# Seven block products in place of eight for the gate and up projections of six feed-forward networks, in split single precision

## The chip, the core and the metric

The kernel runs on one core of one Trainium2 chip. The metric is the device time of the whole program in microseconds. Nothing crosses cores. All data is 32-bit floating point in memory.

## The reference

A sequence of 512 tokens with 1024 channels goes through three layers. Each has a feed-forward network (FFN), a mixer, and a second FFN, so there are six FFNs and three mixers (pooling with latent attention, gated convolution, Fourier mixing with grouped attention), and a last norm.

```
def swiglu(x, w_gate, w_up, w_down):
    return (jax.nn.silu(x @ w_gate) * (x @ w_up)) @ w_down

x = x + 0.5 * swiglu(rms_norm(x, ffn1_norm), w_gate, w_up, w_down)
x = x + mixer(rms_norm(x, mix_norm))
x = x + 0.5 * swiglu(rms_norm(x, ffn2_norm), ...)
```

The inner width is 2816 for the first four FFNs and 2752 for the last two. Gate and up weights are 1024 x width, down weights width x 1024.

## The kernel before

The program runs in nine stages, s = 1 to 9: FFNs are 1, 3, 4, 6, 7 and 9, mixers 2, 5 and 8. Activations are kept with channels on partitions: X is 8 tiles of 128 channels x 512 tokens. A product is made exact enough by splitting each operand into a high part (rounded to the matmul's type) and a low part (the remainder), and adding three matmuls, low x high, high x low and high x high (`mm3`, L379 to L382). The norm's factor per token, r (tile rb), is multiplied in after the matmul; the gain per channel is in Xh and Xl.

Weights come as one long stream of chunks of up to 128 x 1024 numbers (512 KB), in the order in which TensorE wants them (`weight_stream`). SyncE issues one load after another into three raw buffers (`fetch`). ScalarE makes the high part (`high`, the activation on L773), VectorE the low part (`low`, L1126), each into one of three buffers wh and wl. Both engines call `use` at fixed places of their programs, and each call lets them split as far as two chunks ahead of the one in use. Every engine is a queue that is worked off in order; an instruction that waits holds all behind it.

An FFN of before (`ffn`, once for each engine) has 11 groups of 256 inner channels. A group is four chunks: gate for channels 0 to 511 and 512 to 1023 of x, then up in the same way. TensorE sums two 128 x 512 tiles of gate and two of up in four of the eight PSUM banks, the next group in the other four. VectorE multiplies gate by r, ScalarE takes SiLU, VectorE multiplies up by r and both together, ScalarE copies that to Hh and VectorE makes Hl. After all groups `residual` runs the down projection over 22 tiles of H, and the outcome is added to X with factor 0.5; there ScalarE and VectorE also make the next stage's Xh and Xl and the squares for its norm. The norm's statistics come early in the next stage: after the second chunk a matmul sums the squares over channels, VectorE makes the variance (tile small), GpSimd raises it to -0.5 (tile r), VectorE makes a diagonal matrix (tile diag), and TensorE spreads it over partitions after the third chunk, whence ScalarE copies rb. GpSimd does nothing else in an FFN.

Of the kernel before, what the change touches and what calls it, by code (L numbers as in the profile page):

```python
# [17 lines left out]
N_RAW = 3  # L18
AHEAD = 2
# [95 lines left out]
def chunks_ffn(wg, wu, wd):  # L115
    f, got = wg.shape[1], []
    for n0 in range(0, f, 256):
        n1 = min(f, n0 + 256)
        got += chunks(wg, 0, D, n0, n1, 4) + chunks(wu, 0, D, n0, n1, 4)
    return got + chunks_down(wd, f)  # L120


def weight_stream(a):

    got = []
    got += chunks_ffn(a["ffn1_w_gate"][0], a["ffn1_w_up"][0], a["ffn1_w_down"][0])
    wi = a["a_w_in"][0]
    for n0, n1 in ((0, 256), (256, 512), (896, 1024), (1024, 1184), (512, 768), (768, 896)):
        got += chunks(wi, 0, D, n0, n1, 8 if n1 - n0 == 128 else 4)
    got += chunks(a["a_w_pool"][0].rearrange("g c d -> (g c) d"), 0, 512, 0, 128)  # L130
    for n0 in (0, 512):
        got += chunks(a["a_w_kv_up"][0], 0, 256, n0, n0 + 512)
    got += chunks(a["a_w_q_up"][0], 0, 384, 0, 288)
    got += chunks(a["a_w_out"][0], 0, 512, 0, 256)
    for n0, n1 in ((288, 576), (576, 768)):
        got += chunks(a["a_w_q_up"][0], 0, 384, n0, n1)
    for k0 in (0, 512):
        for n0 in range(256 if k0 == 0 else 0, D, 256):
            got += chunks(a["a_w_out"][0], k0, k0 + 512, n0, n0 + 256)
    for w in ("ffn2", "ffn1"):  # L140
        l = 0 if w == "ffn2" else 1
        got += chunks_ffn(a[w + "_w_gate"][l], a[w + "_w_up"][l], a[w + "_w_down"][l])
    for m in range(KT):
        for part in (1, 2, 0):
            n0 = part * D + m * 128
            got += chunks(a["c_w_in"][0], 0, D, n0, n0 + 128, 8)
    got += chunks_down(a["c_w_out"][0], D)
    got += chunks_ffn(a["ffn2_w_gate"][1], a["ffn2_w_up"][1], a["ffn2_w_down"][1])
    got += chunks_ffn(a["ffn1_w_gate_2"], a["ffn1_w_up_2"], a["ffn1_w_down_2"])
    for n0 in (1024, 512, 768, 0, 256):  # L150
        got += chunks(a["w_in_2"], 0, D, n0, n0 + 256, 4)
    got += chunks(a["dft_c"], 0, 128, 0, 256)
    got += chunks(a["dft_cs"], 0, T, 0, T)
    got += chunks(a["dft_ss"], 0, T, 0, T)
    got += chunks(a["fnet_w_2"].rearrange("g c d -> (g c) d"), 0, 512, 0, 128)
    for k0 in (0, 512):
        for n0 in range(0, D, 256):
            got += chunks(a["w_out_2"], k0, k0 + 512, n0, n0 + 256)
    got += chunks_ffn(a["ffn2_w_gate_2"], a["ffn2_w_up_2"], a["ffn2_w_down_2"])
    return got  # L160


def build(nc, a, out):
    ctx = ExitStack()
    with ctx:
# [14 lines left out]
        raw_in = [Event(sem(f"raw_in{i}")) for i in range(N_RAW)]  # L180
# [3 lines left out]
        X = sb("X", [128, KT, T], F)  # L184
        Xh = sb("Xh", [128, KT, T], R)
        Xl = sb("Xl", [128, KT, T], R)
        raw = [sb(f"raw{i}", [128, CAP], F) for i in range(N_RAW)]
        wh = [sb(f"wh{i}", [128, CAP], R) for i in range(N_RAW)]
        wl = [sb(f"wl{i}", [128, CAP], R) for i in range(N_RAW)]
# [7 lines left out]
        rb = [sb(f"rb{i}", [128, T], F) for i in range(2)]  # L197
        sq = [sb(f"sq{i}", [128, T], F) for i in range(2)]
        acc = [sb(f"acc{i}", [128, T], F) for i in range(2)]
# [6 lines left out]
        def scope():  # L206
            place[0] = stage_base
# [6 lines left out]
        stream = weight_stream(a)  # L214

        def parts_of(n, bufs):
            parts, width, _ = stream[n]
            return [bufs[n % N_RAW][0:rows, k0 * width:(k0 + nk) * width] for rows, k0, nk, _ in parts]

        def views(n):  # L220

            _, width, nk = stream[n]
            return [b[n % N_RAW][:, 0:nk * width].rearrange("p (k n) -> p k n", n=width) for b in (wh, wl)]

# [3 lines left out]
        H = [sb(n, [128, 22, T], R) for n in ("Hh", "Hl")]  # L228
        ft = [sb(f"ft{i}", [128, T], F) for i in range(3)]

        scope()
        aRB = sb("a_RB", [128, 10, T], R)
        aQT = [sb(f"a_QT{i}", [128, 2, T], R) for i in range(2)]
        aKT = [sb(f"a_KT{i}", [128, 2, T], R) for i in range(2)]
        aVh, aVl = (sb(n, [128, 4, T], R) for n in ("a_Vh", "a_Vl"))
        aqtm, aktm = (sb(n, [128, 4, 8, 96], F) for n in ("a_qtm", "a_ktm"))
        aP3 = [sb(f"a_P{i}", [128, T], F) for i in range(3)]
        azf = [sb(f"a_zf{i}", [128, T], F) for i in range(2)]
        akrT = sb("a_krT", [32, T], F)
# [10 lines left out]
        aacc = [diag, acc[1]]  # L250
# [10 lines left out]

        scope()
        gRB = sb("g_RB", [128, 8, T], R)
        gKT = sb("g_KT", [128, 2, 2, T], R)
        gVh, gVl = (sb(n, [128, 4, 2, 2, 64], R) for n in ("g_Vh", "g_Vl"))
        gABh, gABl = (sb(n, [128, 4, 4, 256], R) for n in ("g_ABh", "g_ABl"))
        gQT = gABh[:, :, :, :].rearrange("p (i a) (b c) n -> p i (a b) (c n)", i=2, b=2)
        gqtm = sb("g_qtm", [128, 4, 8, 64], F)
# [16 lines left out]
        class Mixer:  # L285
# [3 lines left out]
            def __init__(self, s, causal, ahead, early, fill, P, tiles, stats):  # L289
                self.s, self.causal, self.ahead, self.early, self.fill = s, causal, ahead, early, fill  # L290
                self.P, (self.PTh, self.PTl) = P, tiles
# [18 lines left out]
        mA = Mixer(2, True, 8, 2, (0, 2), aP, (aRB[:, 0:4, :], aRB[:, 4:8, :]), (amx, anb, aL, aLi))  # L310
        mB = Mixer(8, False, 6, 1, (1, 3), gP, (gRB[:, 0:4, :], gRB[:, 4:8, :]), (gmx, gnb, gL, gLi))
# [1645 lines left out]
```

## Time and profile before

| | |
|---|---|
| median of 3 runs | 2810.42 us (2810.4 to 2812.13) |
| the profiled execution | 2811.45 us, span 2809.6 us |
| granted TensorE clock, mean | 0.997 |
| matmuls, and as many weight loads | 12580 |
| read from memory | 249.17 MB, 89 GB/s over the span |

A group of matmul rows has a busy time that counts the overlap of one matmul with the next; the pace of the stream is the distance of their starts. An FFN stage without its neighbours takes about 364 us, and the six together most of the span. The profiled execution is 1 us above the median.

### The profile page before, as it was taken

What the parts mean: (1) busy time and instruction counts of PE and PEld (TensorE: products, weight loads), DVE (VectorE), ACT (ScalarE), POOL (GpSimd) and SP (SyncE); (2) the same over time, 40 slices, a digit from 0 to 9 for tenths busy, and PEclk for the clock granted to TensorE, in tenths of its full rate; (3) what the DMA queues carried; (4) which work ended last, traced back from release to release, by engine and by line L of the source; (5) the groups of instructions that cost most, each with busy time, mean ns of one, the idle gap of its engine ahead of it and who ended that gap; (6) DMA issues with size and microseconds to landing.
All of it is one profiled execution on the core that took longest, in us unless ns stands there. A gap on an engine that the chain in (4) does not pass through costs nothing.

```text
span 2809.6 us, 31389 instructions
## 1 busy us (share of the span) xinstructions
PE 2766.3 (98%) x12580; PEld 2261.5 (80%) x12580; DVE 1331.8 (47%) x1895; ACT 908.2 (32%) x1286; POOL 130.3 (5%) x130
## 2 busy tenths in 40 slices
PE   8999999999999999999999999999999999999998
PEld 6888878888888888888888888888877877788776
DVE  5444358654443444434654444344443557544432
ACT  4222226542322223222233232223222346432221
POOL 0000005300000000000000000000000114000000
PEclk9999999999999999999999999999999999999999
DMA  4332232033323333333333333333322320233322
GB/s 152 99 98 91 91 86 77 24 89 103 95 92 96 96 98 90 101 96 96 98 90 98 98 90 98 92 95 91 105 85 89 92 81 23 61 103 100 90 84 70
DMA packets 282704, 253.30 MB, mean 90 GB/s; under 512 B 8384, under 2 KB 278848, under 8 KB 282560
## 3 DMA queue, kind: packets, MB, share of 16 engines
q1 hardware_dynamic: 282560, 251.30, 29.9%
q8 instruction: 101, 1.65, 0.2%
q14 instruction: 43, 0.35, 0.0%
HBM read 249.17 MB, written 2.10 MB: 89 GB/s over the span
## 4 chain that ended last, share of the span: by engine, by line
PE 82%; issue 13%; DVE 3%; ACT 2%; DMA 0%; SPq 0%; POOLq 0%; POOL 0%; DVEq 0%
PE bank L380 27%; PE bank L381 27%; PE bank L382 27%; PE bank L469 1%; DVE a_mx L1235 0%; PE bank L433 0%; PE bank L422 0%; DMA raw<-in_ffn_w_gate 0%; DVE wl L1126 0%; ACT Xh L804 0%; DVE a_nb L1142 0%; ACT wh L773 0%; DVE a_KT L1138 0%; ACT a_P L857 0%; DVE X L1135 0%
## 5 line engine op out<-in xcount | busy, mean ns | idle before, releaser
L1126 DVE TENSOR_TENSOR wl<-raw,wh 128x1024 fp32r<-128x1024 f32 (+6 forms) x498 | 573.9, 1166 | 976.2 <-ACT wh L773 975.3
L380 PE MATMUL bank<-Xh,wl 128*128 128x512 f32 x2544 | 997.6, 392 | 12.9 <-DVE wl L1126 10.6
L382 PE MATMUL bank<-Xh,wh 128*128 128x512 f32 x2544 | 992.0, 390 | 0.0
L381 PE MATMUL bank<-Xl,wh 128*128 128x512 f32 x2544 | 991.5, 390 | 0.0
L773 ACT ACTIVATE wh<-raw 128x1024 fp32r<-128x1024 f32 (+6 forms) x498 | 494.9, 1009 | 1001.3 <-PE bank L382 994.9
L380 PEld LDWEIGHTS bank<-Xh,wl 128*128 128x128 f32 x2544 | 476.3, 187 | 117.0 <-issue 12.6
L381 PEld LDWEIGHTS bank<-Xl,wh 128*128 128x128 f32 x2544 | 476.4, 187 | 102.9 <-issue 1.9
L382 PEld LDWEIGHTS bank<-Xh,wh 128*128 128x128 f32 x2544 | 476.1, 187 | 103.0
L380 PE MATMUL bank<-Hh,wl 128*128 128x512 f32 x1056 | 419.0, 397 | 0.0
L382 PE MATMUL bank<-Hh,wh 128*128 128x512 f32 x1056 | 417.0, 395 | 0.0
L381 PE MATMUL bank<-Hl,wh 128*128 128x512 f32 x1056 | 417.0, 395 | 0.0
L1135 DVE TENSOR_TENSOR ft<-bank,rb 128x512 f32<-128x512 f32 x264 | 181.6, 688 | 168.7 <-PE bank L382 117.8
L380 PEld LDWEIGHTS bank<-Hh,wl 128*128 128x128 f32 x1056 | 197.9, 187 | 54.3 <-issue 6.6
L382 PEld LDWEIGHTS bank<-Hh,wh 128*128 128x128 f32 x1056 | 197.9, 187 | 48.6
L381 PEld LDWEIGHTS bank<-Hl,wh 128*128 128x128 f32 x1056 | 197.9, 187 | 47.5
L804 ACT ACTIVATE Hh<-ft 128x512 fp32r<-128x512 f32 x132 | 83.8, 635 | 269.2 <-DVE ft L1135 269.2
L841 ACT ACTIVATE ft<-ft 128x512 f32<-128x512 f32 x132 | 83.6, 633 | 209.3 <-DVE ft L1135 209.2
L1135 DVE TENSOR_TENSOR Hl<-ft,Hh 128x512 fp32r<-128x512 f32 x132 | 91.4, 692 | 92.5 <-ACT Hh L804 92.5
L1135 DVE TENSOR_TENSOR ft<-ft,ft 128x512 f32<-128x512 f32 x132 | 91.4, 692 | 4.5
L1678 POOL TENSOR_TENSOR r<-small,half 128x4 f32<-128x4 f32 x10 | 10.1, 1014 | 1758.5 <-DVE small L1144 1758.5
L801 ACT ACTIVATE Xh<-X,par 128x512 fp32r<-128x512 f32 x64 | 46.0, 725 | 130.4 <-DVE X L1138 110.6
L1138 DVE SCALAR_TENSOR_TENSOR Xl<-X,par,Xh 128x512 fp32r<-128x512 f32 x64 | 47.6, 751 | 44.5 <-ACT Xh L801 44.5
(264 smaller groups left out, 1583.5 us busy)
## 6 DMA issues: line engine op xcount, KB each, us to landing
raw<-in_ffn_w_gate SPq DMA_DIRECT2D x128, 512.0 KB, 3.8
raw<-in_ffn_w_up SPq DMA_DIRECT2D x128, 512.0 KB, 3.9
raw<-in_ffn_w_down SPq DMA_DIRECT2D x114, 512.0 KB, 3.5
raw<-in_c_w_in SPq DMA_DIRECT2D x24, 512.0 KB, 3.7
raw<-in_w_in SPq DMA_DIRECT2D x10, 512.0 KB, 3.8
raw<-in_a_w_in SPq DMA_DIRECT2D x8, 512.0 KB, 3.8
raw<-in_a_w_out SPq DMA_DIRECT2D x8, 512.0 KB, 3.5
raw<-in_c_w_out SPq DMA_DIRECT2D x8, 512.0 KB, 3.5
```

The costliest lines, as they stand in the source:

```text
L380: e.matmul(o, ll, rh, start=start, stop=False)
L381: e.matmul(o, lh, rl, start=False, stop=False)
L382: i = e.matmul(o, lh, rh, start=False, stop=stop)
L469: e.transpose(bank[0:rows, t * 128:(t + 1) * 128], src, ident).then_inc(mm.up(name), 1)
L773: e.activation(hi, src, ACT.Copy).then_inc(whi.up(("w", n)), 1)
L801: e.activation(Xh[:, t, :], X[:, t, :], ACT.Copy, scale=col(gain, t)).then_inc(act.up(("xh", s, t)), 1)
L804: e.activation(dst, src, ACT.Copy, scale=scale).then_inc(act.up(*names), 1)
L841: e.activation(B[0:wd, :], A[0:wd, :], ACT.Silu).then_inc(act.up(("silu", s, ht)), 1)
L1126: e.tensor_tensor(lo, src, hi.bitcast(F), ALU.subtract).then_inc(wlo.up(("w", n)), 1)
L1135: e.tensor_tensor(dst, a, b, op).then_inc(dve.up(*names), 1)
L1138: e.scalar_tensor_tensor(dst, a, scalar, b, op0, op1).then_inc(dve.up(*names), 1)
L1678: e.tensor_tensor(dst, a, b, op).then_inc(pool.up(*names), 1)
```

## The change

For gate and up of an FFN the weights are seen as a block matrix: A11 and A12 are the gate weights of 256 inner channels for x channels 0 to 511 and 512 to 1023, A21 and A22 those of up. x is cut in the same way into channels (first and second half) and tokens (0 to 255, 256 to 511), blocks B11, B12, B21, B22. A product of 2 x 2 blocks has 8 block products; here it is made with 7, over sums of blocks (S1 to S4 of the weights, T1 to T4 of x) and with sums of results. The first of the 11 groups stays as it was. The ten others are "jobs"; each product has 4 k-tiles x 2 halves x 3 terms and 256 columns.

- x sums: ScalarE makes X times gain into ya and yb (8 copies), VectorE the four sums T1 to T4, and both their high and low parts, at the start of each FFN while the first group is on TensorE. T4 goes to a place in Xh and Xl.
- weight sums: host code stores the blocks of the ten jobs contiguously, 128 x 1024 numbers each (4 KB a partition). SyncE loads A11, A21 (for S1), A12, A11 or A21 (for S3) and A22 as plain loads, five per job. GpSimd issues transfers that add a block of memory onto a raw buffer: S1 = A21 + A22, then S2 = S1 + A11 and S4 = S2 + A12 in the same buffer after the split of what stood there, and S3. Six raw buffers, four wh and four wl.
- results: three PSUM banks a job (a, b, c). ScalarE seeds bank b with a copy of product 1 and takes three snapshots (snapC, snapU, snapV) between products; TensorE waits for them before products 2, 6, 7, 3 and 4. VectorE adds and multiplies by r in 8 operations of 512 columns. Product 1 of a job is made in the middle of the one before, but for the first jobs of the two runs, so that jobs 3 and 9 are "alone" with six products.
- the down projection is made in two parts: over 8 tiles of H after job 3, over 14 after job 9; H has 14 places for 22 tiles. Each part is added to X.
- the widths 2752 are padded with zeros to 2816. One buffer less each of rb and acc; the mixers' tiles move to other addresses. The ring for GpSimd's transfers is set to 1024 bytes a partition.

```
+PRODUCT = {1: ("a", "A11", "B11"), 2: ("b", "A12", "B21"), 3: ("c", "S4", "B22"), 4: ("a", "A22", "T4"),
+           5: ("c", "S1", "T1"), 6: ("a", "S2", "T2"), 7: ("a", "S3", "T3")}
+def products(i):
+    if alone(i):
+        return [(i, p) for p in (5, 6, 2, 7, 3, 4)]
+    return [(i, 5), (i, 2), (i, 6), (i + 1, 1), (i, 7), (i, 3), (i, 4)]
+SLOT = {"A11": (0, 0), "A12": (1, 1), "S3": (2, 2), "A22": (3, 3), "S1": (4, 5), "S2": (4, 5), "S4": (4, 5)}
+SUMS = {"S1": ("A21", "A22"), "S2": (None, "A11"), "S3": ("A11", "A21"), "S4": (None, "A12")}
...
+    def run(self, s, i0, i1):
+        self.product(s, i0, 1)
+        for i in range(i0, i1):
+            for j, p in products(i):
+                self.product(s, j, p)
+        self.load_block(s, i0, "A11")
+        self.load_block(s, i0, "S1")
+        self.load_block(s, i0, "A12")
+        for i in range(i0, i1):
+            if i + 1 < i1:
+                self.load_block(s, i + 1, "A11")
+            self.load_block(s, i, "S3")
+            if i + 1 < i1:
+                self.load_block(s, i + 1, "S1")
+            self.load_block(s, i, "A22")
+            if i + 1 < i1:
+                self.load_block(s, i + 1, "A12")
...
+            def product(s, i, p):
+                role, _, operand = PRODUCT[p]
+                n, h, l, _ = chunk()
+                no = job_bank(role, i)
+                bank = take(no, (role, s, i)) if p in (1, 5) else banks[no]
...
+                if p in (2, 6):
+                    w.wait_ge(act, ("seed", s, i))
+                elif p == 7:
+                    w.wait_ge(act, ("snapU", s, i))
+                elif p == 3:
+                    w.wait_ge(act, ("snapC", s, i))
+                elif p == 4:
+                    w.wait_ge(act, ("snapV", s, i))
...
+                for k in range(4):
+                    xh, xl = x_operand(k, operand, 0), x_operand(k, operand, 1)
+                    for m in range(2):
...
+                        e.matmul(o, l[:, k, sl], xh, start=start, stop=False, skip_group_check=True)
+                        e.matmul(o, h[:, k, sl], xl, start=False, stop=False, skip_group_check=True)
+                        ins = e.matmul(o, h[:, k, sl], xh, start=False, stop=last, skip_group_check=True)
```

ScalarE's part of a job; `use` splits the weights three products ahead:

```
+                def job(i):
+                    for j, p in products(i):
+                        if (j, p) == (i, 5):
+                            use()
+                            if i == 0 or alone(i - 1):
+                                seed(i)
+                            if i > 0 and not alone(i - 1):
+                                silu(i - 1, 1)
+                        elif (j, p) == products(i)[1]:
+                            use()
+                            if i > 0:
+                                w.wait_ge(dve, ("h", s, i - 1))
+                            snap(snapC, "c", i, "snapC", 5)
+                            if i > 0 and not alone(i - 1):
+                                tail(i - 1)
+                        elif (j, p) == products(i)[3 if not alone(i) else 2]:
+                            if i > 0:
+                                w.wait_ge(dve, ("right", s, i - 1))
+                            snap(snapU, "a", i, "snapU", 6)
+                            use()
+                        elif p == 7:
+                            use()
+                            if not alone(i):
+                                seed(i + 1)
+                            silu(i, 0)
+                        elif p == 3:
+                            snap(snapV, "a", i, "snapV", 7)
+                            use()
+                        else:
+                            use()
```

GpSimd's part of an FFN:

```
+            def ffn(s):
+                def add(name, i):
+                    base, added = SUMS[name]
+                    slot, landed = SLOT[name][i % 2], sum_event(name, i)
+                    if base:
+                        w.wait_ge(raw_in[slot], (name, s, i))
+                    else:
+                        before = "S1" if name == "S2" else "S2"
+                        w.wait_ge(landed, (before, s, i))
+                        w.wait_ge(wlo, ("w", stream.op_of[before, s, i]))
+                    e.dma_start(raw[slot][:, :], stream.block[s, i, added], accum_op=ALU.add).then_inc(landed.sem, 16)
...
+                norm(s)
+                add("S1", 0)
+                for i in range(JOBS):
+                    if i == EARLY + 1:
+                        add("S1", i)
+                    add("S3", i)
+                    if not alone(i):
+                        add("S1", i + 1)
+                    add("S2", i)
+                    add("S4", i)
```

## Rows read from the trace of the kernel before

**Rows 1.** The page: span, TensorE's busy time, the chain by engine.

```profile
span 2809.6 us, 31389 instructions
...
PE 2766.3 (98%) x12580; PEld 2261.5 (80%) x12580; DVE 1331.8 (47%) x1895; ACT 908.2 (32%) x1286; POOL 130.3 (5%) x130
...
PE 82%; issue 13%; DVE 3%; ACT 2%; DMA 0%; SPq 0%; POOLq 0%; POOL 0%; DVEq 0%
```

**Rows 2.** TensorE's waits, longest: total us, times, longest.

```profile
PE bank L380 <- DVE wl L1126: 10.6, 2, 9.9
```

**Rows 3.** Busy time by stretch: us, PE, PEld, DVE, ACT, POOL, clock, DMA share.

```profile
620.00:642.00 22.00, 22.00 (x99) 18.22 (x98) 10.17 (x12) 6.56 (x8) 0.00 (x0) 1.00 0.33 98
```

**Rows 4.** TensorE's timeline in gate/up: start, us, line, operation.

```profile
699.72 0.39 PE L382 MATMUL bank<-Xh,wh 128*128 128x512 f32 x1
...
705.84 0.39 PE L382 MATMUL bank<-Xh,wh 128*128 128x512 f32 x1
```

**Rows 5.** TensorE's timeline in stage 8, 256 columns.

```profile
2235.79 0.28 PE L382 MATMUL bank<-wh,Xh 128*128 128x256 f32 x1
...
2242.99 0.28 PE L382 MATMUL bank<-wh,Xh 128*128 128x256 f32 x1
...
2272.47 0.28 PE L380 MATMUL bank<-wh,g_RB 128*128 128x256 f32 x1
...
2277.91 0.28 PE L381 MATMUL bank<-wl,g_RB 128*128 128x256 f32 x1
```

**Rows 6.** TensorE's timeline, a matmul over 64 rows and the next.

```profile
2792.74 0.50 PE L380 MATMUL bank<-Hh,wl 64*128 64x512 f32 x1
2793.08 0.39 PE L381 MATMUL bank<-Hl,wh 64*128 64x512 f32 x1
```

**Rows 7.** Groups by form, 620 to 642: busy us, mean ns.

```profile
L1126 DVE TENSOR_TENSOR wl<-raw,wh 128x1024 fp32r<-128x1024 f32 x4 | 4.8, 1224 | 7.6 <-ACT wh L773 7.6
L773 ACT ACTIVATE wh<-raw 128x1024 fp32r<-128x1024 f32 x4 | 4.1, 1053 | 7.8 <-PE bank L382 7.8
L1135 DVE TENSOR_TENSOR ft<-bank,rb 128x512 f32<-128x512 f32 x4 | 2.8, 688 | 2.5 <-PE bank L382 1.8 <-ACT ft L841 0.8
...
L841 ACT ACTIVATE ft<-ft 128x512 f32<-128x512 f32 x2 | 1.3, 632 | 3.2 <-DVE ft L1135 3.2
```

**Rows 8.** VectorE's timeline at the start of stage 3.

```profile
587.56 0.16 DVE L1144 TENSOR_SCALAR small<-bank 128x4 f32<-128x4 f32 x1 [2.12 <-PE bank L422]
588.88 0.69 DVE L1135 TENSOR_TENSOR diag<-par,r 128x512 f32<-128x512 f32 x1 [1.16 <-POOL r L1678]
```

**Rows 9.** ScalarE's timeline there: rb, and the table load before SiLU.

```profile
594.02 0.60 ACT L804 ACTIVATE rb<-bank 128x512 f32<-128x512 f32 x1 [6.13 <-PE bank L433]
...
597.53 1.28 ACT L841 ACT_TABLE_LOAD   x1 [1.96 <-DVE ft L1135]
```

**Rows 10.** TensorE after its last down matmul, and two stretches with clock.

```profile
2795.97 1.02 PE L422 MATMUL bank<-ones,acc 128*128 128x1 f32 x8 [2.27 <-DVE acc L1135]
...
2796.00:2800.00 4.00, 1.93 (x9) 1.41 (x10) 0.86 (x2) 0.00 (x0) 1.01 (x1) 0.80 0.00 0
...
480.00:490.00 10.00, 8.40 (x45) 7.28 (x46) 7.66 (x31) 6.88 (x20) 9.34 (x10) 0.83 0.12 36
```

**Rows 11.** Transfers: two stretches, then issues with KB, us to landing.

```profile
10.00:12.00 2.00, 2.00 (x5) 1.61 (x6) 1.15 (x2) 1.00 (x2) 0.00 (x0) 1.00 1.06 417
12.00:14.00 2.00, 2.00 (x7) 1.56 (x7) 1.91 (x3) 2.00 (x5) 0.00 (x0) 1.00 1.01 389
...
raw<-in_ffn_w_gate SPq DMA_DIRECT2D x128, 512.0 KB, 3.8
...
par<-in_par SPq DMA_DIRECT2D x1, 763.5 KB, 8.6
...
gain<-in_par SPq DMA_DIRECT2D x1, 4.0 KB, 1.8
```

**Rows 12.** GpSimd's timeline, the norm of stage 3.

```profile
587.81 1.04 POOL L1678 TENSOR_TENSOR r<-small,half 128x4 f32<-128x4 f32 x1 [42.41 <-DVE small L1144]
```

More of the change, by code:

```diff
@@ L112, in chunks_down, with __init__ @@
     return [c for n0, n1, per in DOWN for c in chunks(w, 0, f, 128 * n0, 128 * n1, per)]
[L115 to L120, printed above, removed]
+class Load:
+    def __init__(self, name, slot, parts, width, after):
+        self.name, self.slot, self.parts, self.width, self.after = name, slot, parts, width, after
+class Weights:
+    def __init__(self, slot, load, total, parts, width, nk):
+        self.slot, self.load, self.total, self.parts, self.width, self.nk = slot, load, total, parts, width, nk
+        self.buf = self.before = self.stage = self.due = None
@@ L231, in build @@
+        aP3 = [sb(f"a_P{i}", [128, T], F) for i in range(3)]
+        assert place[0] <= at_XT
+        scope(at_XT)
+        aqtm, aktm = (sb(n, [128, 4, 8, 96], F) for n in ("a_qtm", "a_ktm"))
         scope()
+        aCh, aCl = (sb(n, [128, KT, T], R) for n in ("a_Ch", "a_Cl"))
         aRB = sb("a_RB", [128, 10, T], R)
@@ new lines, in ffn @@
+            def ffn(s):
+                hooks = [nothing, *stats(s, 7, 7)]
+                for side in ("gate", "up"):
+                    proj([(FIRST_BANK[side, m], (side, s, m)) for m in range(2)], [128, 128], KT, Xh, Xl, x_ready(s), hooks)
+                mm.also(("plain", s))
+                for i in range(JOBS):
+                    if i == 0 or i == EARLY + 1:
+                        product(s, i, 1)
+                    for j, p in products(i):
+                        product(s, j, p)
+                    if i == EARLY:
+                        down(s, 0)
@@ L777, in use @@
                     used[0] += 1
-                    while split[0] < min(used[0] + AHEAD, len(stream)):
+                    while split[0] < len(ops) and used[0] >= ops[split[0]].due:
                         high()
@@ L1130, in use @@
                     used[0] += 1
-                    while split[0] < min(used[0] + AHEAD, len(stream)):
+                    while split[0] < len(ops) and used[0] >= ops[split[0]].due:
                         low()
@@ new lines, in job @@
+                def job(i):
+                    before = i > 0 and not alone(i - 1)
+                    use()
+                    if before:
+                        first_half_h(i - 1)
+                        times_r(i - 1, 1)
+                    use()
+                    if before:
+                        second_half_h(i - 1)
+                    use()
+                    if alone(i):
+                        low_h(i - 1)
+                        use()
+                        left(i)
+                        use()
+                        times_r(i, 0)
+                        lower_right(i)
+                        use()
+                        right(i)
+                    else:
+                        left(i)
+                        use()
+                        if before:
+                            low_h(i - 1)
+                        use()
+                        times_r(i, 0)
+                        use()
+                        lower_right(i)
+                        use()
+                        right(i)
@@ L1839, in sync_program @@
             e.dma_start(par[:, :], a["par"]).then_inc(par_in.sem, 16)
-            for n in range(2, len(stream)):
-                fetch(n)
+            for load in stream.loads[2:]:
+                fetch(load)
             for t in range(KT):
```

607 lines of the change are left out of this document (440 added, 167 removed).

## The prediction

> **What bounds the kernel now.** I read the page's busy table and its chain first. TensorE is busy for 2766.3 of 2809.6 us and its matmuls are 82% of the chain; the 13% of "issue" is time in which it waited for nothing that the profile shows [rows 1]. The waits of TensorE then say whether anyone holds it up: its largest releaser is VectorE's weight split with 10.6 us, 9.9 of them one wait at the start [rows 2]. The stage view of one gate/up group shows TensorE busy for all 22.0 us at full clock, VectorE for 10.17, ScalarE for 6.56, the DMA engines for 0.33 [rows 3]. So the six FFNs run at TensorE's own pace, and fewer or cheaper matmuls shorten the run only while splits, PSUM reads and transfers keep up.
>
> **The matmuls.** Of 11 gate/up groups of an FFN, ten become "jobs". A group is 2 sides x 8 k-tiles x 2 halves x 3 split terms = 96 matmuls of 512 columns; a job is 7 products x 4 x 2 x 3 = 168 of 256 columns. Starts 27 apart in a gate/up stretch are 699.72 and 705.84, so 0.2267 us each, 21.76 a group [rows 4]. For 256 columns two stretches are there: 60 steps from 2235.79 to 2242.99, 0.1200, and 46 steps from 2272.47 to 2277.91, 0.1183 [rows 5]. Half the columns thus cost a little over half, with a fresh weight load for each. I take 0.119: a job is 20.0 us and saves 1.77, with ends 1.60 and 1.89. Sixty jobs: **-106 us** (-96 to -113). Down projections keep their number; the padding of D_FF 2752 to 2816 turns 16 matmuls over 64 rows into full ones, whose followers start 0.34 instead of 0.23 us later now [rows 6]: -2.
>
> A rule speaks against the change. The Trainium skill (TensorE: Matmul & The Clock Gate, Back-to-back issue gap) gives about 81 ns for a stream of pairs of load and matmul at 128 columns and 131 ns at 512. By it a group would be 12.6 us and a job, at an estimated 98 ns, 16.5: 234 us slower over 60 jobs. The trace does not agree, it has 227 ns at 512 columns [rows 4]; the sum goes by the rows, and what the rule would do here is the fifth rival.
>
> **What the other engines get.** A split of 1024 columns is 1.22 us on VectorE and 1.05 on ScalarE, an operation on 512 columns 0.69 and 0.63 [rows 7]. A job has 7 splits in place of 4. VectorE: 7 splits and the low half of H, 8 x 1.22, and 8 operations of 512 (two multiplications by r, two for H, left, lower_right, two in right): 9.8 + 5.5 = 15.3 of 20.0 us. ScalarE: 8 x 1.05 + 6 x 0.63 (three snapshots, the seed, two SiLUs) = 12.2. Both fit, so in the middle of a run they cost nothing; if VectorE took 30% more per job it would be the bound.
>
> **The opening of each FFN is where cover ends.** Let t=0 be the first matmul. The variance comes at 587.56 in the third stage, two chunks (48 matmuls, 10.9) after its start, so its start is 576.3; the diagonal ends at 13.3 and rb is written from 17.7 [rows 8, 9]. Now VectorE must, in its order, after the diagonal: 4 sums of x (4.9), split S1 (1.2), gate times r (1.4), T1 and T2 low (2.4), split A12 (1.2), T3 low (1.2), SiLU times r (1.2), times up (1.4): 14.9, and about 1 for hand-overs (S1 first has to be summed, SiLU has a table load of 1.28 [rows 9]): h at 29.2. Only then does ScalarE copy h (1.05), make T4 (1.05), split S2 (1.05) and A11 of job 1 (1.05) and write the seed (0.63): 34.0. TensorE wants the seed for product 2 at 21.8 + 2 x 2.86 = 27.5. So it stands for about 6.5 to 7 us in each FFN: **+42**. Ends: 3 each if some hand-overs overlap, 9 if each operation waits for the one on the other engine. An idle TensorE loses clock: after 2.3 idle us, some matmuls and 2 more idle us the clock reads 0.80, then 0.50; a stretch of 10 us in which TensorE was busy for 8.40 reads 0.83 [rows 10], a third of it at the 1.2 GHz level and the rest at 2.4, which loses 1.7 us of work. Once an FFN: **+10** (0 to 20).
>
> **The adding transfers.** No row shows one. Each job has 5 plain loads and 4 adding ones of 512 KB, issued from GpSimd, whose queue was idle in FFNs apart from the norm. Adding in place has to read the block and the buffer. A plain 512 KB load lands in 3.8 us, a 4 KB one in 1.8, and the DMA engines at a share of 1.0 moved 389 to 417 GB/s [rows 11]; I take 390, 1.34 us for 512 KB. From below, an adding transfer is a plain one, 3.8 us. From above, the 763.5 KB load in a full queue, 8.6 us [rows 11]. I take 1.8 + 2 x 1.34 = 4.5, with hand-over 4.7, nearer to the plain one since the blocks are contiguous. A job then uses the DMA engines for 5 x 1.34 + 4 x 2.68 = 17.4 of 20.0 us.
>
> The Trainium skill (Collectives: The Full Stack, The bandwidth ceiling: the fold count and why AG ≠ RS ≠ AR) says the same for reductions: the sum itself is free, two source reads halve the rate. By its 62.28 and 32.35 GB/s the second factor would be 1.93 in place of 2, an estimate of 17.1 us per job. No run here shows it yet.
>
> S2 is made from S1 in the same buffer, S4 from S2, each after the split before it, and the buffer serves every second job. That makes a loop: low split of S4(i-1), base load of S1(i+1) (3.5), its addition issued (1.0, as GpSimd's small operation [rows 12]), and behind it in the same queue S2(i) (4.7, and 1.7 behind the other's data), splits (2.5), S4(i) (4.7), splits (2.5): 20.6 us against 20.0. ScalarE and VectorE wait in order for each sum, and snapU, which product 7 wants, stands behind the split of S4. The first jobs have 1 to 5 us in hand, so this costs about 0.5 us an FFN: **+3**. In the two "alone" jobs S2 has one product less of time; at 4.7 us snapU is about 0.3 us late: **+4**. These two terms grow fast: above 5 us an adding transfer each further us adds 2 us to the loop and 2 us to an alone job.
>
> The down projection in two parts adds no matmul; 8 more PSUM reads of 0.69 us lie under 43 us of matmuls. The deeper buffers (4 for weights, 6 raw) are at no cost. Mixers keep their order with tiles at other addresses: 0, and +5 at worst.
>
> **The sum** against the profiled 2811.45 us: -106 - 2 + 42 + 10 + 3 + 4 = -49: 2762. The median of the runs before is 1 us lower than that execution, which changes nothing.
>
> **Rivals.**
> First, the loop of sums is the bound; this one ends slower. Place: ScalarE at the splits of S2 and S4, and through snapU TensorE at product 7. If an adding transfer takes 6 us in the midst of the other loads, the loop is 20.6 + 2 x 1.3 = 23.2 us; some 6 jobs per FFN pay 3.2 us each, less the 5 us in hand per FFN, 36 x 3.2 - 30 = 85, and the alone jobs 12 x 2.6 = 31: 2878. At 7 us it is 25.2, 157 and 55: 2974. It turns slower than before from about 5.3 us. For it: a DMA share of 17.4 of 20, and the 8.6 us of a load in a full queue. Against: the median landing of 3.8 us [rows 11]. Chance 0.32, mostly 2815 to 2900.
> Second, the same in weaker form, 5 to 5.3 us: 2782 to 2811. Chance 0.13.
> Third, adding transfers cost as plain ones (-7, the last two terms), the openings overlap to 3 us (-24), and 256 columns take 0.1183 (-7): 2724. For it: some hand-overs of my serial count may run side by side. Chance 0.10.
> Fourth, the change doesn't do what it says: beside dense transfers 256 columns take 0.125, a job 21.0, and only 46 us are saved: 2822. No row has such transfers beside it. Chance 0.02.
> Fifth, weight loads pace a stream of short matmuls: 2261.5 us over 12580 loads are 0.180 each [rows 1], a job would be 30.2 us, 8.4 more than a group: 3315. In [rows 5] each matmul had its load and took 0.119. Chance 0.01. By the figures of the Trainium skill's page on TensorE above it would be 234 us more than before, 3045.
>
> **How the numbers follow.** The forecast, 2740 to 2785, has 0.42. A measurement can tell a change from none from about 0.2%, 5.6 us. Faster holds the forecast, the third rival and most of the second: 0.62. Within 0.2% lie the ends of the second and first: 0.07. Slower: 0.31. The range leaves out half of the third rival and the far tail of the first: 2732 to 2875.
>
> **What would show it.** Right: 256-column matmuls 0.119 us apart; one wait of TensorE of 6 to 7 us per FFN on ScalarE's seed; job stretches of 20 us with VectorE at three quarters; adding transfers landing in under 5 us. Wrong: waits on weight splits or snapshots in each job, DMA share near 1, job stretches of over 21.8 us.

## The result and the profile after

The changed kernel takes 3198.11 us (3196.51 to 3202.9) against 2810.41 for the kernel before: a ratio of 1.138, with a 95% interval of 1.136 to 1.140. It is 13.8% slower, where 1.7% faster was forecast, and it lies above the range. These are lines of its page: span, busy time by engine, clock and DMA share in 40 slices, and the chain by engine.

```profile
span 3195.9 us, 41047 instructions
...
PE 2819.9 (88%) x16900; PEld 2531.1 (79%) x16900; DVE 1664.1 (52%) x2209; ACT 1229.8 (38%) x1696; POOL 341.1 (11%) x370
...
PEclk9898999989989989999998998998988999989999
DMA  6567432155673465753326576346575220365652
...
PE 9%; issue 5%; DMA 4%; DVE 3%; ACT 2%; POOL 0%; POOLq 0%; DVEq 0%; SPq 0%; ACTq 0%
```

Against [rows 1] TensorE's busy time is up by 54 us and its idle time by 333, from 43 to 376. No engine is full, the DMA engines are at half to three quarters in the FFNs, and the clock, 0.997 before, dips in every FFN (mean 0.937). The chain, which [rows 1] had at 82% on TensorE, is no help here: it was followed back only to 2434 us, and its shares sum to 23%. When nothing is full, a wait that goes round is the thing to look for. TensorE's waits name two ends of one (total us, times, longest):

```profile
PE bank L652 <- DVE wl L1458: 200.4, 48, 5.7
PE bank L652 <- ACT snapU L1050: 60.8, 38, 5.0
PE bank L652 <- ACT bank L1050: 46.0, 12, 7.2
PE bank L652 <- DVE XT L1467: 15.4, 5, 5.0
```

In [rows 2] the largest was 10.6. The third line holds the forecast's seed wait, 5.7 to 7.2 us once an FFN, and six shorter ones. The first is new, 48 waits of some 4 us on a weight split: about one per job. The page's groups (busy and mean ns, then idle before and its releaser) and its transfers (KB, us to landing) say what the splits waited for:

```profile
L1019 ACT ACTIVATE wh<-raw 128x1024 fp32r<-128x1024 f32 (+1 forms) x668 | 677.0, 1034 | 1228.2 <-DMA raw<-in_blocks 736.5
...
raw<-in_blocks SPq DMA_DIRECT2D x300, 512.0 KB, 5.5
raw<-in_blocks POOLq DMA_DIRECT2D x240, 512.0 KB, 7.4
```

ScalarE stood 736.5 us before splits for transfers of blocks. An adding transfer lands in 7.4 us (median), where 4.7 was taken, and a plain load in 5.5, where [rows 11] had 3.8.

One job of FFN 1 shows the circle. First the job's stretch between two copies of snapU (us, busy of PE, PEld, DVE, ACT, POOL, clock, DMA share, GB/s), then GpSimd's timeline (start, us, operation, idle before), then ScalarE's, then VectorE's:

```profile
247.41:274.65 27.24, 22.92 (x170) 22.57 (x169) 14.25 (x16) 11.00 (x16) 3.52 (x4) 0.87 0.72 174
```

```profile
253.64 1.78 POOL L2175 DMA_DIRECT2D raw<-in_blocks  x2 [3.98 <-DMA raw<-in_blocks]
267.43 0.86 POOL L2175 DMA_DIRECT2D raw<-in_blocks  x1 [12.00 <-DVE wl L1458]
276.57 0.86 POOL L2175 DMA_DIRECT2D raw<-in_blocks  x1 [8.27 <-DMA raw<-in_blocks]
280.27 1.78 POOL L2175 DMA_DIRECT2D raw<-in_blocks  x2 [2.83 <-DVE wl L1458]
```

```profile
264.51 2.00 ACT L1019 ACTIVATE wh<-raw 128x1024 fp32r<-128x1024 f32 x2 [10.72 <-DMA raw<-in_blocks]
...
272.26 0.60 ACT L1050 ACTIVATE snapC<-bank 128x512 f32<-128x512 f32 x1 [2.50 <-DVE S L1467]
272.75 1.05 ACT L1050 ACTIVATE Hh<-S 128x1024 fp32r<-128x1024 f32 x1
273.70 1.05 ACT L1019 ACTIVATE wh<-raw 128x1024 fp32r<-128x1024 f32 x1
274.65 0.59 ACT L1050 ACTIVATE snapU<-bank 128x512 f32<-128x512 f32 x1
275.13 2.00 ACT L1019 ACTIVATE wh<-raw 128x1024 fp32r<-128x1024 f32 x2
```

```profile
247.54 1.23 DVE L1458 TENSOR_TENSOR wl<-raw,wh 128x1024 fp32r<-128x1024 f32 x1 [2.56 <-ACT wh L1019]
...
265.60 1.23 DVE L1458 TENSOR_TENSOR wl<-raw,wh 128x1024 fp32r<-128x1024 f32 x1 [9.95 <-ACT wh L1019]
...
271.54 0.69 DVE L1467 TENSOR_TENSOR S<-snapC,S 128x512 f32<-128x512 f32 x1
274.79 1.23 DVE L1458 TENSOR_TENSOR wl<-raw,wh 128x1024 fp32r<-128x1024 f32 x1 [2.56 <-ACT wh L1019]
...
278.80 1.22 DVE L1458 TENSOR_TENSOR wl<-raw,wh 128x1024 fp32r<-128x1024 f32 x1
```

At 253.64 GpSimd issues S1 of the next job and, right behind it at 254.2, S2 of this one. S2 lands at 264.5, 10.3 us later. ScalarE has stood at S2's split for 10.72 us by then, and all that is queued behind it waits too: A11, SiLU and S3, snapC (which needs h of the last job from VectorE, busy without a gap until 272.2), the high part of h, and at 273.70 the split of S4, 9.2 us after S2's. S4's own addition was issued at 267.43 and landed 5.8 us later, at 273.2, so it only just doesn't add. Behind S4's split come A22's and S1's; S1's low part ends at 280.0, and only then may S2 of the next job be added to the same buffer: issued at 280.8, 7.1 us after 273.70. The circle is 10.3 + 9.2 + 7.1 = 26.6 us, and the next S2 takes 11.0 to land; jobs are 27.2 to 27.5 us apart. TensorE isn't in it. It idles 4.3 us in this turn.

The forecast's own loop closes in the same turn. The low part of the S4 before ends at 248.8, the base load that it frees lands at 253.2, S1 is issued at 253.64 and S2 at 254.2, S2 lands at 264.5, S4 is issued at 267.43 and lands at 273.2, and its low part ends at 276.0: 27.2 us. The two circles share S2's landing. Beside it they run within half a us of each other: S4 has landed at 273.2 and ScalarE is free for it at 273.70; the base load of the next S1 to be added lands at 279.8, and the low part of the S1 on which S2 waits ends at 280.0. This timeline alone can't say which of them holds, and the experiments take them apart.

At the start of FFN 3 TensorE's timeline shows the forecast's wait, with the clock behind it:

```profile
674.09 0.36 PE L652 MATMUL bank<-XT,wl 128*128 128x256 f32 x1 [3.86 <-DVE XT L1467]
...
685.41 0.55 PE L652 MATMUL bank<-Xh,wl 128*128 128x256 f32 x1 [6.81 <-ACT bank L1050]
685.76 0.41 PE L653 MATMUL bank<-Xl,wh 128*128 128x256 f32 x1
685.97 0.41 PE L654 MATMUL bank<-Xh,wh 128*128 128x256 f32 x1
...
685.40:688.80 3.40, 3.39 (x16) 3.40 (x17) 2.34 (x3) 1.32 (x2) 0.86 (x1) 0.50 0.37 45
```

After 6.81 idle us the matmuls start 0.21 us apart at a clock of 0.50, its 1.2 GHz level. The wait for T1 ahead of it is one that the forecast didn't have: the first addition of the FFN, issued at 658.61, landed only after 10.7 us, and ScalarE stood 8.2 us at its split.

### The profile page after: what moved, and what is told of

Its sections match the earlier page's. It is cut to its first block and busy times, and to the rows that moved or that the text cites. A ratio compares the mean times of both kernels' runs of the same rounds, so it can differ in the third digit from the quotient of the medians.

```text
span 3195.9 us, 41047 instructions
## 1 busy us (share of the span) xinstructions
PE 2819.9 (88%) x16900; PEld 2531.1 (79%) x16900; DVE 1664.1 (52%) x2209; ACT 1229.8 (38%) x1696; POOL 341.1 (11%) x370
## 5 line engine op out<-in xcount | busy, mean ns | idle before, releaser
L1458 DVE TENSOR_TENSOR wl<-raw,wh 128x1024 fp32r<-128x1024 f32 (+1 forms) x668 | 797.4, 1198 | 1198.1 <-ACT wh L1019 1197.0
L1019 ACT ACTIVATE wh<-raw 128x1024 fp32r<-128x1024 f32 (+1 forms) x668 | 677.0, 1034 | 1228.2 <-DMA raw<-in_blocks 736.5
L652 PE MATMUL bank<-XT,wl 128*128 128x256 f32 x1440 | 471.1, 327 | 277.4 <-DVE wl L1458 200.4
L652 PE MATMUL bank<-Xh,wl 128*128 128x256 f32 x1920 | 551.3, 287 | 46.3 <-ACT bank L1050 46.0
L652 PEld LDWEIGHTS bank<-XT,wl 128*128 128x128 f32 x1440 | 329.5, 229 | 295.3 <-ACT wh L1019 245.1
L653 PE MATMUL bank<-Xl,wh 128*128 128x256 f32 x1920 | 548.6, 286 | 0.0
L654 PE MATMUL bank<-Xh,wh 128*128 128x256 f32 x1920 | 547.0, 285 | 0.0
L653 PE MATMUL bank<-XT,wh 128*128 128x256 f32 x1440 | 459.3, 319 | 0.0
L654 PE MATMUL bank<-XT,wh 128*128 128x256 f32 x1440 | 458.1, 318 | 0.0
L653 PEld LDWEIGHTS bank<-XT,wh 128*128 128x128 f32 x1440 | 331.3, 230 | 0.0
L654 PEld LDWEIGHTS bank<-XT,wh 128*128 128x128 f32 x1440 | 329.9, 229 | 0.0
L566 PE MATMUL bank<-Xh,wl 128*128 128x512 f32 x496 | 200.1, 403 | 18.7 <-DVE wl L1458 14.5
```

Of the source, the lines that this page charges most:

```text
L566: e.matmul(o, ll, rh, start=start, stop=False)
L652: e.matmul(o, l[:, k, sl], xh, start=start, stop=False, skip_group_check=True)
L653: e.matmul(o, h[:, k, sl], xl, start=False, stop=False, skip_group_check=True)
L654: ins = e.matmul(o, h[:, k, sl], xh, start=False, stop=last, skip_group_check=True)
L1019: e.activation(hi, src, ACT.Copy).then_inc(whi.up(("w", n)), 1)
L1458: e.tensor_tensor(lo, src, hi.bitcast(F), ALU.subtract).then_inc(wlo.up(("w", n)), 1)
```

## The experiments

All edits are to the changed kernel unless "the kernel before" is named. e7_down2 has ten executions, v3_opening and v4_queue four each; every other time is that of one execution. The kernel before took 2810.5 to 2811.2 us beside them. "Job" is the distance of snapU's starts in FFN 1, jobs 5 to 8.

### Is it the additions?

e2_noadd leaves them out, and splits what the base load brought (the weights are then wrong, the rest as it was):

```
 def add(name, i):
+    return
...
-    w.wait_ge(sum_event(op.total[0], op.total[2]), op.total)
+    w.wait_ge(raw_in[op.slot], ("S3" if op.total[0] == "S3" else "S1", *op.total[1:]))
```

> GpSimd issues no transfer; S1, S2 and S4 are split from the block A21 as loaded, S3 from A11, so the outputs are not the reference's. All products, splits, snapshots and plain loads stay. Theory (only the loop of sums makes the difference to the forecast): jobs take 20.0 to 20.5 us, the seed's wait of 6.8 us stays in each FFN, whole about 2770 us. Rival (256-column products, snapshots or VectorE are themselves too slow): jobs stay at 22 us or more, whole 2900 or more.

2768.52 us, job 20.0. Its busy row, its longest wait of TensorE, and a job's stretch:

```profile
PE 2678.5 (97%) x16900; PEld 2407.6 (87%) x16900; DVE 1677.9 (61%) x2209; ACT 1245.9 (45%) x1696; POOL 130.1 (5%) x130
...
PE bank L652 <- ACT bank L1050: 35.0, 6, 7.2
...
224.56:244.60 20.04, 20.04 (x170) 20.04 (x169) 14.36 (x16) 11.29 (x14) 0.00 (x0) 1.00 0.41 132
```

All that the additions don't touch came as forecast: a job of 20.04 at full clock, 88 us less busy time than [rows 1], one seed wait per FFN (4.5 to 7.2 us, 35.0 in all). The additions cost the other 430 us.

e1_plain keeps the transfers and only drops the sum:

```
-e.dma_start(raw[slot][:, :], stream.block[s, i, added], accum_op=ALU.add).then_inc(landed.sem, 16)
+e.dma_start(raw[slot][:, :], stream.block[s, i, added]).then_inc(landed.sem, 16)
```

> GpSimd's four transfers of a job copy the second block over the first instead of adding it, so the outputs are not the reference's; number, bytes from memory, order and waits stay. Theory (the loop of sums is the bound, and an adding transfer is slow since it reads two sources): a GpSimd transfer lands in about 4.5 us in place of 7.4, a job falls from 26.9 to about 22 us, the whole to about 2950 us. Rival (transfers issued by GpSimd are slow whatever they do, or wait behind other loads): landing stays above 6.5 us and the time near 3150.

2896.56 us, job 21.3 to 22.8, landing 4.6 us (median). So the chain costs 128 us with plain transfers too; that they add costs 302 more. Both theories stood too high. GpSimd's issues, and ScalarE's splits of S2 and of S4, in one job:

```profile
241.75 1.05 POOL L2175 DMA_DIRECT2D raw<-in_blocks  x2 [2.87 <-DVE wl L1458]
...
264.52 1.06 POOL L2175 DMA_DIRECT2D raw<-in_blocks  x2 [3.31 <-DVE wl L1458]
```

```profile
248.87 2.01 ACT L1019 ACTIVATE wh<-raw 128x1024 fp32r<-128x1024 f32 x2 [6.24 <-DMA raw<-in_blocks]
...
258.06 1.05 ACT L1019 ACTIVATE wh<-raw 128x1024 fp32r<-128x1024 f32 x1
```

S2, the second of each pair, is issued at 242.3 and split 6.6 us later, S4 is split 9.2 us after it, and the next S2 goes out 7.0 us after that, at 265.0: 22.8 us, the job. S4's transfer had landed at 255.4, 2.7 us before its split, so it isn't in this circle.

### What does a transfer cost alone?

e8_probe is the kernel before with transfers of GpSimd into spare buffers, one after another or several at a time, of another kind in each FFN; SyncE's loads of the FFN go on beside them:

```
+kind = dict(accum_op=ALU.add) if add else {}
...
+e.dma_start(probe[i][:, c0:c1], a["ffn1_w_gate"][0][128 * i:128 * i + 128, c0:c1], **kind).then_inc(
+    event.sem, 16)
...
+w.wait_ge(probe_in[i], HERE)
```

> The kernel of before, with GpSimd transfers of 512 KB into spare buffers that nobody reads, each waited for: FFN 1 plain one at a time, FFN 3 adding one at a time, FFN 4 adding 256 KB, FFN 6 adding two at a time, FFN 7 adding four of 256 KB at a time, FFN 9 plain two at a time. Theory (an adding transfer by itself costs 1.8 us and twice the data time): 4.7 us adding, 3.8 plain, 3.3 at half size; two at a time 7.4. Rival (adding is slow by itself, over 3 data times): 6 us or more alone. In either case the whole stays within 1% of before, as the DMA engines are a third busy.

2808.74 us. Issues (KB, us to landing), in order: plain, adding, adding by half, adding in pairs, plain in pairs:

```profile
probe<-in_ffn_w_gate POOLq DMA_DIRECT2D x12, 512.0 KB, 4.2
...
probe<-in_ffn_w_gate POOLq DMA_DIRECT2D x24, 512.0 KB, 5.5
...
probe<-in_ffn_w_gate POOLq DMA_DIRECT2D x24, 256.0 KB, 4.3
...
probe<-in_ffn_w_gate POOLq DMA_DIRECT2D x22, 512.0 KB, 8.3
...
probe<-in_ffn_w_gate POOLq DMA_DIRECT2D x24, 512.0 KB, 4.6
```

The adding one lies between the theory's 4.7 and the rival's 6; all other kinds took longer than the theory said. Half the bytes save 1.2 us, so 512 KB are 2.4 of data and 3.1 of fixed time, if the time is a fixed part and one in proportion to the bytes. The data is what was forecast (2.68), the fixed part isn't (1.8, from a 4 KB load of SyncE's). Two additions at once take 8.3 us (median of all), two plain transfers 4.6: the additions take 2.8 us more than one by one, a little over one's data time. Four adding halves at once take 5.5 us. The Trainium skill (DMA: Bandwidth & Descriptors, Anatomy of one DMA — SWDGE (gpsimd) path) has a fixed part of about 2.0 us and 436 GB/s for transfers from GpSimd, an estimate of 3.2 us for 512 KB; the plain ones here took 4.2.

### Which link is the circle?

The prediction's loop ran through the buffer that S1, S2 and S4 share, used by every second job. e4_three gives a third, so that S1's base load needn't wait for it:

```
-"S1": (4, 5), "S2": (4, 5), "S4": (4, 5)
+"S1": (4, 5, 6), "S2": (4, 5, 6), "S4": (4, 5, 6)
```

> A third raw buffer for the chain S1, S2, S4, so that the base load of S1(i+1) no longer waits for the split of S4(i-1); the queue's order is as in the changed kernel. Theory (the loop through the shared buffer sets 26.9 us): what is left is S2, split, S4, and the in-order splits of S4, A22 and S1, 2 x 7.4 + 2.5 + 3.5 = 21 us a job, whole about 2870. Rival (the additions themselves fill the DMA engines): a job stays over 25 us, whole above 3080.

3137.74 us, job 25.8 to 27.6: 60 us of 430. The time lies in the rival's range, and e10_loose below speaks against the rival's reason. Taking the base load out of one circle leaves the other, which is nearly as long: S2 still took 9.7 to 11.6 us to land.

e3_order only issues S2 of a job ahead of S1 of the next:

```
     add("S3", i)
+    add("S2", i)
     if not alone(i):
         add("S1", i + 1)
-    add("S2", i)
```

> Only the order in GpSimd's queue changes: S2 of job i is added before S1 of job i+1. Theory (half of S2's 10 us is its place behind another addition in the queue): S2 lands in 6 to 7 us, a job takes about 23.5 us, whole about 3020. Rival (the DMA engines as a whole are the bound, 18.9 us of their time per job in bursts): jobs stay within 1 us of 26.9, whole above 3150.

3023.39 us, job 22.6 to 24.3: 175 us, as expected. S2 lands in 6.6 to 8.2 us. e5_both has both edits.

> Third buffer and S2(i) added before S1(i+1). Theory: the two effects overlap, as both shorten the same loop: about 20.5 to 21 us a job, whole 2800 to 2850, at best as before. Rival (they are separate bottlenecks): the gains add, 3198 - 175 - that of the third buffer alone, below 2750.

3008.82 us, job 22.7 to 24.2. A miss for the expectation: the two gains don't join into the whole. Its stretch, then GpSimd's issues (here S2 is the first of each pair) and ScalarE's splits of S2 and of S4:

```profile
250.98:274.50 23.52, 21.83 (x168) 21.66 (x168) 14.25 (x16) 11.14 (x16) 3.52 (x4) 0.93 0.83 200
```

```profile
256.90 1.78 POOL L2175 DMA_DIRECT2D raw<-in_blocks  x2 [3.34 <-DVE wl L1458]
...
280.41 1.77 POOL L2175 DMA_DIRECT2D raw<-in_blocks  x2 [2.01 <-DVE wl L1458]
```

```profile
264.36 2.01 ACT L1019 ACTIVATE wh<-raw 128x1024 fp32r<-128x1024 f32 x2 [6.45 <-DMA raw<-in_blocks]
...
273.55 1.05 ACT L1019 ACTIVATE wh<-raw 128x1024 fp32r<-128x1024 f32 x1
```

The circle read above accounts for it: in e5_both S2 is issued at 256.90 and its split starts at 264.36 (7.5 us, in place of 10.3), S4's split starts at 273.55 (9.2) and the next S2 goes out at 280.41 (6.9): 23.5 us, the job. The last two terms are as they were, since they are the work of two engines in order. e1_plain has them too, 9.2 and 7.0. Over the three runs S2's time goes from 10.3 to 7.5 and 6.6 us, the rest of the circle changes by 0.3 us at most, and the circle is 26.6, 23.5 and 22.8.

e10_loose cuts the circle and keeps the traffic. The four additions of a job stay, with their bytes; those of S2 and S4 go to a spare buffer, and the splits of S2 and S4 wait for S1's sum only (so S2 and S4 have S1's values):

```
-before = "S1" if name == "S2" else "S2"
-w.wait_ge(landed, (before, s, i))
-w.wait_ge(wlo, ("w", stream.op_of[before, s, i]))
+slot, landed = 6, sum_in[3]
...
+w.wait_ge(landed, HERE)
```

> The same four adding transfers a job with the same bytes, but those of S2 and S4 go to a spare buffer that nobody reads and follow each other only; S2 and S4 are split from the buffer of S1, so the outputs are not the reference's. S1 and S3 stay true sums. Theory A (the bound is the chain of dependence: S2 issued, landed, split, S4 issued, landed, then in order the splits of S4, A22 and S1, and S2 of the next job; 7.3 + 2.9 + 6.2 + 7 = 23.4 us in the run with both changes): jobs near 20.5 us, whole 2770 to 2830. Theory B (the traffic itself is the bound, DMA share 0.80 of 23.6 us = 18.9 us a job): jobs stay above 22.5 us, whole above 2930.

2794.3 us; a job's stretch, and GpSimd's transfers:

```profile
210.00:230.04 20.04, 20.04 (x170) 20.04 (x169) 14.57 (x17) 11.37 (x15) 3.25 (x4) 1.00 0.96 240
...
raw<-in_blocks POOLq DMA_DIRECT2D x240, 512.0 KB, 7.9
```

The transfers take even longer, 7.9 us, the DMA engines are at 0.96, and the job is 20.04 us. Neither the bytes nor the landing time by itself is the bound; it is that a landing stands in a circle. The edit takes both S2's and S4's landing out, and so cuts both circles. That it is S2's which counts is from e1_plain, e3_order and e5_both. Together they settle the main cause.

e6_half adds only half the columns of each block (the other half of the weights keeps the base's values):

```
-e.dma_start(raw[slot][:, :], stream.block[s, i, added], accum_op=ALU.add).then_inc(landed.sem, 16)
+e.dma_start(raw[slot][:, 0:512], stream.block[s, i, added][:, 0:512], accum_op=ALU.add).then_inc(landed.sem, 16)
```

> The changed kernel with each adding transfer over half the columns only (256 KB; the other half stays the base block, so the outputs are not the reference's). Alone such a transfer lands in 4.3 us, 1.3 less than the whole. Theory (chain with two additions a job, and S2 behind another in the queue): a job takes 2 x 1.3 + 1.3 = 3.9 us less than 26.9, about 23, whole 2960 to 3010. Rival (traffic): DMA time falls by 5.4 of 18.9 us a job and the time with it in proportion, jobs at PE's 20, whole below 2800.

2952.41 us, 8 below the range expected, with a median landing of 4.7 and jobs of 23.5 to 25.3. It is 56 us above e1_plain at nearly the same median, but the median isn't S2's: behind S1, S2 landed in 7.0 to 7.9 us here and in 5.2 to 6.6 in e1_plain. In one of the turns read, S1's base load landed late as well, and the next S2 went out 9.1 us after S4's split and not 7.1. This is read from FFN 1 alone.

### The part that was to cost nothing

e7_down2 is the kernel before with its down projection in two parts, after group 4 and at the end:

```
+if j == 4:
...
+    for t0, t1, _ in DOWN:
+        proj([((4 + t) % 8, ("part", s, t)) for t in range(t0, t1)], [128] * (t1 - t0), 8, *H, ready0, None)
```

> The kernel of before with only the down projection in two parts, over tiles 0 to 7 of H after the fifth group and over the rest at the end. Theory of the prediction: no matmul added, the 8 additional PSUM reads lie under matmuls: within 0.2% of before, 2806 to 2816 us. Rival (part of the loss is there: waits for H or banks at the seams, shorter chunks): 1 to 3 us per FFN more, 2817 to 2830.

2810.19 against 2810.6 us, a ratio of 1.000 (0.999 to 1.001). It costs nothing.

### Versions without the circle

v1_gpsum makes all sums on GpSimd as tensor additions, from four plain loads a job:

```
-e.dma_start(raw[slot][:, :], stream.block[s, i, added], accum_op=ALU.add).then_inc(landed.sem, 16)
...
+tt(*(raw[SLOT[b][i % 2]][:, :] for b in (dst, x1, x2)), ALU.add, (name, s, i))
```

> The same seven products, but the four sums of a job are GpSimd tensor additions of blocks already loaded (four loads per job, no adding transfer, a second buffer for A22). A 128x256 addition on GpSimd took 0.74 us before, so one of 1024 columns should take 2.9 and four 11.7 of 20 us. Theory (only the latency of the sums was wrong): each sum is ready 3.1 us after the split before it, jobs take 20 to 20.5 us, whole 2765 to 2780. Rival (GpSimd and VectorE slow each other on shared tiles' ports): additions of 4 us or more, VectorE's splits above 1.4 us, jobs over 22 us, whole above 2850.

2939.45 us, job 22.7: the rival's side, though one addition takes GpSimd 2.6 us and not 4. VectorE is slowed beside it. GpSimd's timeline, then two lines of VectorE's, a split that overlaps a GpSimd addition and one that doesn't:

```profile
238.19 5.15 POOL L2140 TENSOR_TENSOR raw<-raw,raw 128x1024 f32<-128x1024 f32 x2 [4.25 <-DVE wl L1454]
```

```profile
241.11 3.31 DVE L1454 TENSOR_TENSOR wl<-raw,wh 128x1024 fp32r<-128x1024 f32 x1 [2.56 <-ACT wh L1015]
...
244.95 1.21 DVE L1454 TENSOR_TENSOR wl<-raw,wh 128x1024 fp32r<-128x1024 f32 x1
```

Such a split has two inputs in SBUF. The Trainium skill (SBUF — State Buffer, Who interferes with whom) says that such an instruction of VectorE contends with one of GpSimd's that reads SBUF; the trace agrees (3.31 us against 1.21). How much of the longer job is due to that, no run separates.

v2_mixed keeps the additions by transfer where nothing is chained to them closely (S1 and S3), and lets VectorE make S2 and S4 behind its low split of S1 and S2:

```
+if op.total and op.total[0] in ("S1", "S2"):
...
+    w.wait_ge(raw_in[slot], (added, s, i))
...
+    tt(raw[op.slot][:, :], raw[op.slot][:, :], raw[slot][:, :], ALU.add, (name, s, i))
```

> S1 and S3 by adding transfers as before, S2 and S4 by VectorE from the blocks already loaded (two tensor additions of 1024 columns right behind the low splits of S1 and S2), so no transfer stands between two splits. VectorE has 15.3 + 2.4 = 17.7 us of a job's 20.0. Theory A (chain): jobs at 20 to 20.7 us, whole 2770 to 2800. Theory B (what remains is that VectorE is too full, or two adding transfers still hold up the splits): jobs over 21.8, whole above 2811.

2957.79 us, job 25.0 to 25.5: another miss, with a circle of another kind. SyncE's waits (total, times, longest):

```profile
SPq L73 <- DVE raw L1476: 1081.6, 108, 20.3
```

SyncE loads in order, and A11 of the next job stood ahead of S3's and S1's base loads. A11's buffer is free only once S2 has been summed from it; S3 then comes too late, and S2 of the next job with it. v4b_queue_only changes this order alone:

```
 for i in range(i0, i1):
-    if i + 1 < i1:
-        self.load_block(s, i + 1, "A11")
     self.load_block(s, i, "S3")
     ...
     if i + 1 < i1:
+        self.load_block(s, i + 1, "A11")
         self.load_block(s, i + 1, "A12")
```

> v2_mixed (S2 and S4 by VectorE) with SyncE's order of loads changed: base of S3, base of S1 of the next job, A22, and only then A11 and A12 of the next job, as A11's buffer is now held until S2 is added. Theory (v2_mixed waits at the split of S3, whose base load stands behind A11's wait): jobs go from 25.5 to 20 to 20.7 us, whole 2780 to 2805. Rival (VectorE, 17.7 of 20 us, is too full): above 2850.

2794.17 us, job 20.0: one load moved, 164 us.

v3_opening is v2_mixed with the start of an FFN in another order: ScalarE makes S2's split and the seed ahead of SiLU, the copies of h and T4 come after.

```
-                use()
+                use(2)
+                seed(0)
```

> As v2_mixed, and at the opening of each FFN the seed of job 0 and the split of S2 come before SiLU, T3 and T4, and the copy of the first H and T4 after the split of A11 of job 1. The wait of 6.8 us before product 2 should fall to under 1.5 us, the rest of the opening stays: 5 to 6 us less per FFN, 30 to 35 in all against v2_mixed, whole about 2745 to 2765 (0.977 to 0.984 of before). Rival (the opening is bound by the sum of VectorE's work, and the wait only moves to product 6 or 7): 10 us less at most, 2770 or more.

2930.56 us, 27 less than v2_mixed. The seed wait is gone from TensorE's waits; the gain is a little under the 30 to 35 us expected, and the whole lies far above its range, which took for granted that v2_mixed would be fast.

v4_queue has both, v4b's loads and v3's opening:

> The same with the opening of v3_opening. Theory: 27 us less than v4b_queue_only, as between v2_mixed and v3_opening; 2755 to 2780, ratio to before 0.980 to 0.989. Rival: VectorE's backlog at the opening eats it, ratio 0.99 to 1.01.

```profile
PE 2681.1 (97%) x16900; PEld 2403.0 (87%) x16900; DVE 1807.2 (65%) x2329; ACT 1239.2 (45%) x1696; POOL 235.4 (8%) x250
...
PE bank L653 <- ACT snapU L1051: 27.7, 24, 2.3
...
226.25:246.29 20.04, 20.04 (x171) 20.04 (x170) 16.63 (x18) 11.38 (x15) 1.74 (x2) 1.00 0.71 183
```

2778.53 us (2775.97 to 2782.21), a ratio of 0.989 (0.987 to 0.991): 1.1% faster than the kernel before. Seven products do pay once the sums hold nobody up. The lines are its busy row, its longest wait of TensorE, and a job. The seed wait of 39.5 us in v4b_queue_only is gone here, but 20 us came back as waits on snapU, and the gain is 16 us, not 27.

## Why the prediction was wrong

- **Matmuls (-106): right.** 20.04 us a job in e2_noadd, e10_loose and v4_queue, where 20.0 was forecast.
- **Seed wait (+42): right.** 5.7 to 7.2 us at the opening of each FFN in the changed kernel and 35.0 in all in e2_noadd, where 6.5 to 7 each was forecast.
- **The rest of the sum: right.** Without the two terms of the adding transfers it gives 2755; e2_noadd, which has none, took 2768.5. With all four and no circle, e10_loose took 2794.3. Down in two parts is free (e7_down2).
- **Size of an adding transfer (4.7): wrong.** One at a time it is 5.5, and 7.4 in the kernel. The step took SyncE's 1.8 us for a 4 KB load as the fixed part of GpSimd's transfers, where 3.1 was measured, and held 1.7 us enough for a neighbour in the queue, which makes 6.4 for S2. Of a pair each took 8.3, and S2, issued right behind S1, 10.3 in the turn shown.
- **The loop (20.6 us): the step that failed, in its sizes and in its links.** With the sizes of the turn shown it doesn't come to 20.6 but to 27.2, the job: base load 4.4 (3.5 forecast), issues 1.0 (1.0), S2 10.3 (6.4), splits 2.9 (2.5), S4 5.8 (4.7), splits 2.8 (2.5). And it wasn't the only loop. The other has one landing, S2's, and 16.3 us of other engines' work, which stands behind S2's split in ScalarE's order and ahead of the next S2 in VectorE's. The prediction said that "ScalarE and VectorE wait in order for each sum" and didn't put into a loop what they had queued behind it. Even with the 6.4 us that it took for S2, this circle is 22.7 us. e1_plain is nearly that case: S2 in 6.6, a job of 22.8, and 128 us above e2_noadd. The other 302 us came with the longer landings of adding transfers. e4_three took the base load out of the forecast's loop and gained 60 us.
- **The slack: wrong.** The first rival had the mechanism, at a chance of 0.32. But by its own formula 7.4 us gives a loop of 26.0, 36 x 6.0 - 30 = 186, with 12 x 5.4 = 65 for the alone jobs, thus 2762 + 186 + 65 = 3013 and not 3198. It let 6 jobs of 10 pay, less 5 us in hand. The stages say otherwise: from the norm of FFN 3 to that of FFN 4 it is 427.7 us after and 355.4 in e2_noadd, 72.3 more, opening included, which is ten times the 7.2 by which a job of FFN 1 is longer. In a circle, work in hand is not refilled: sixty jobs at 7.2 us are 432 of the 430 us. The range left out what it called the far tail of this rival, and ended at 2875.
- **The clock (+10): too small by far, but little of it counts.** Busy time of TensorE is 141 us above e2_noadd's for the same matmuls, as the clock falls behind the stalls (0.50, the 1.2 GHz level, behind the seed wait, 0.87 over the job shown). In that job it is 2.9 us, yet the circle doesn't run through TensorE, and a faster clock would only have made the idle time longer. This is read from one job's timelines; no run separates it.
- **DMA time (17.4 of 20 us): a little low.** e10_loose has 0.96 of 20.04, 19.2 us. It was counted as evidence for the rival; e10_loose shows that a share of 0.96 costs the job nothing.

Of its own signs for being wrong, the waits on splits in each job and jobs over 21.8 us came; a DMA share near 1 didn't, and the cause wasn't there.

Open: why an addition takes 7.4 us in the kernel and not 5.5 (pairs explain some of it), whether S4's landing would hold the changed kernel if ScalarE came to its split sooner (no run frees S4's alone), and the 26 us between e10_loose and e2_noadd, of which TensorE's waits show 6.8 more on the seed and 12.4 on the sums of x.

## What to carry to other kernels

When a transfer is issued only after an engine has finished with the last one's result, follow the circle through everything that each in-order queue holds between the two, not only through the data; if its sum is over the period, every turn pays and slack doesn't help. Look for more than one such circle: here two were nearly equally long, so that taking a link out of one gained 60 us of 430. Don't judge a transfer in a chain by its bytes or the DMA share, but by its time to landing behind its neighbours in the queue, measured with the very kind that is planned. Before giving up on a transfer-heavy change, take its chained transfers off the chain and check the order of loads against who holds their buffers: here this made 13.8% slower into 1.1% faster.

## What the runs showed of the hardware

- An adding transfer of GpSimd's, 512 KB: 5.5 us one at a time (3.1 fixed, 2.4 of data) against 4.2 for a plain one; two at once 8.3 against 4.6 (e8_probe, with SyncE's loads beside them).
- Beside additions, plain loads of SyncE's slow down too: 5.5 us in the changed kernel, 4.4 in e1_plain beside plain transfers of GpSimd's, 3.6 in e2_noadd.
- A VectorE split of 128 x 1024 with both inputs in SBUF went from 1.21 to 3.31 us beside a GpSimd addition of the same size, itself 2.6 (v1_gpsum).
- TensorE kept 20.04 us a job at full clock with the DMA engines at 0.96 and 240 GB/s (e10_loose).
